# The first two weight items of the feed-forward stage: gate then up, or turn by turn

## The reference

```
x = x + rms_norm(mix, norm_w[1])
h = rms_norm(x, norm_w[2])
ff = (silu(h @ w_gate) * (h @ w_up)) @ w_down      # w_gate, w_up: 1024 x 2816, w_down: 2816 x 1024
x = x + rms_norm(ff, norm_w[3])
```

## Time and profile before

| | |
|---|---|
| median of 3 runs | 2828.58 us (2825.28 to 2828.79) |
| the profiled execution: its time, its span | 2831.39 us, 2829.6 us |
| PE busy | 2705.1 us, 96% of the span |
| DVE, ACT, POOL busy | 1829.3, 1115.9, 1227.8 us |
| granted TensorE clock, mean | 0.973 |

### The profile page before, as it was taken

How to read it: one execution, slowest core, us unless ns; L and a number is a source line. 1 busy time by engine, 2 the same in 40 slices (tenths; PEclk the granted TensorE clock), 3 DMA queues, 4 the chain that set the end, 5 groups by cost and what they waited for, 6 DMA issues and landing times. The chain is left out here.

```text
span 2829.6 us, 36052 instructions
## 1 busy us (share of the span) xinstructions
PE 2705.1 (96%) x12868; PEld 2175.8 (77%) x12868; DVE 1829.3 (65%) x2886; ACT 1115.9 (39%) x2094; POOL 1227.8 (43%) x776
## 2 busy tenths in 40 slices
PE   7999999999799999999989999999997999999997
PEld 5677877778588888888766788777785888888886
DVE  4479865583766566666654798545738656666666
ACT  4336434573523222333333364336744322233323
POOL 1228410340656544565433284103316654466545
PEclk9999999899899999999999999998998999999999
DMA  4103310433111211111330123105231121111113
GB/s 134 45 23 90 112 60 25 141 90 112 38 60 47 73 45 44 46 58 59 128 102 23 31 91 111 60 18 155 90 111 39 53 67 45 44 51 53 59 59 127
DMA packets 186881, 199.30 MB, mean 70 GB/s; under 512 B 19312, under 2 KB 162800, under 8 KB 186496
## 3 DMA queue, kind: packets, MB, share of 16 engines
q1 hardware_dynamic: 180992, 176.63, 20.1%
q10 hardware_dynamic: 5760, 20.97, 1.9%
HBM read 158.78 MB, written 38.80 MB: 70 GB/s over the span
## 5 line engine op out<-in xcount | busy, mean ns | idle before, releaser
L2178 POOL TENSOR_TENSOR ring_lo<-ring_sum,ring_hi 128x512 fp32r<-128x512 f32 x212 | 318.9, 1519 | 500.8 <-ACT ring_hi L2259 500.8
L2395 PE MATMUL ps<-form_hi,ring_hi 128*128 128x512 f32 x1232 | 484.3, 393 | 27.2 <-issue 14.5
L2395 PE MATMUL ps<-form_lo,ring_hi 128*128 128x512 f32 x1232 | 482.5, 392 | 0.0
L2395 PE MATMUL ps<-form_hi,ring_lo 128*128 128x512 f32 x1232 | 482.2, 391 | 0.0
L901 PE MATMUL ps<-act_hi,whi 128*128 128x512 f32 x960 | 395.9, 412 | 9.2 <-ACT smr L441 8.4
L2259 ACT ACTIVATE ring_hi<-ring_sum 128x512 fp32r<-128x512 f32 x212 | 132.7, 633 | 641.1 <-DVE ring_sum L2464 641.1
L901 PE MATMUL ps<-act_lo,whi 128*128 128x512 f32 x960 | 379.2, 395 | 0.0
L901 PE MATMUL ps<-act_hi,wlo 128*128 128x512 f32 x960 | 379.2, 395 | 0.0
L2507 DVE TENSOR_TENSOR yacc<-yacc,ps 128x1024 f32<-128x1024 f32 x176 | 214.8, 1220 | 243.4 <-PE ps L2421 243.4
L1316 DVE TENSOR_SCALAR_CACHE_REDUCE ties<-score,kth 128x384 uint8<-128x384 f32 (+5 forms) x396 | 348.4, 942 | 4.8
L604 POOL TENSOR_TENSOR wlo<-raw,whi 128x1024 fp32r<-128x1024 f32 x56 | 137.1, 2448 | 408.7 <-ACT whi L646 408.7
(11 more groups left out here) (323 smaller groups left out, 4731.3 us busy)
## 6 DMA issues: line engine op xcount, KB each, us to landing
raw<-in_w_in SPq DMA_DIRECT2D x56, 512.0 KB, 3.8
ff_raw<-in_w_gate SPq DMA_DIRECT2D x22, 1024.0 KB, 5.4
ff_raw<-in_w_up SPq DMA_DIRECT2D x22, 1024.0 KB, 5.3
ff_raw<-in_w_down SPq DMA_DIRECT2D x22, 1024.0 KB, 5.1
proj_scratch<-stage ACTq DMA_DIRECT2D x40, 512.0 KB, 2.7
wc<-proj_scratch SPq DMA_DIRECT2D x14, 1280.0 KB, 6.7
xmid_scratch<-xres SPq DMA_DIRECT2D x16, 512.0 KB, 2.6
resid<-xmid_scratch SPq DMA_DIRECT2D x16, 512.0 KB, 6.4
```

The lines of the kernel that those rows point to most:

```text
L2178: pool.tensor_tensor(flat_form(ring_lo[slot]), src, flat_form(ring_hi[slot]).bitcast(F32), ALU.subtract)\
L2395: mm = pe.matmul(ps[:, PRODUCT_BANK[i], :], w[:, k], a[:, k], start=(k == 0 and m == 0), stop=(k == 3 and m == 2))
```

## The change

The first gate item and the first up item become one sequence of fourteen products, `OPENING`, with f as its place: G0, G1, U0, U1, G2, G3, G4, U2, U3, U4, G5, G6, U5, U6 (f = 0 to 13). T7 stands between U0 and U1. The up item has the banks 4 to 7 of PSUM for its products, where the transposes of the tiles are written too (even tiles in 4 and 5, odd ones in 6 and 7): U0 waits for tile 6 to be copied out, U2 for tile 7. Both items take their raw blocks, each from its own buffer. The tables OPENING_SUM, OPENING_DRAIN, OPENING_STEP and OPENING_PIECE give the counts of semaphores for the new order. From H0 on every queue has its old order.

What moves on the other engines:
- DVE sums the weight forms in the order of f, makes `form_lo3` of the earlier tiles itself (POOL did), and drains G1, U1 and G2 between its token forms.
- ACT copies G0 and U0 out before the high parts of the token forms 5 and 6.
- POOL makes fourteen `ring_lo` in the order of f; the zeroing of `yacc` stands after f = 11, and waits for `form_lo6`.
- SP loads the second gate block after twelve `ring_lo`, not seven.

```diff
-            t_lo_p = sig("t_lo_p", 3)
-            t_lo_v = sig("t_lo_v", 7)
+            t_lo_p = sig("t_lo_p", 2)
+            t_lo_v = sig("t_lo_v", 8)
+            TOKENS_READY = {2: 3, 3: 4, 4: 6, 5: 7, 6: 8}
...
+            OPENING = ((0, 0), (0, 1), (1, 0), (1, 1), (0, 2), (0, 3), (0, 4), (1, 2), (1, 3), (1, 4), (0, 5), (0, 6), (1, 5), (1, 6))
+            OPENING_SUM = {(0, 1): 1, (1, 1): 2, (0, 2): 3, (0, 3): 4, (0, 4): 5, (1, 2): 6, (1, 3): 7, (1, 4): 8, (0, 6): 9, (1, 6): 10}
...
+            opening = lambda r: isinstance(r, int) and r < 2
+            summed = lambda r, i: OPENING_SUM[r, i] if opening(r) else 5 * r + SUMMED[i]
+            drained = lambda r, i: OPENING_DRAIN[r, i] if opening(r) else 10 * r + DRAINED[i]
+            step_done = lambda r, n: OPENING_STEP[r][n] if opening(r) else 10 * r + n
+            piece_done = lambda r, n: OPENING_PIECE[r][n] if opening(r) else 10 * r + (1, 7, 8, 10)[n]
+            product_bank = lambda r, i: 4 + PRODUCT_BANK[i] if opening(r) and r == 1 else PRODUCT_BANK[i]
...
+            def first_sum(v, f):
+
+                s, i = OPENING[f]
+                v.wait_ge(*f_in[s](L, 16))
+                if f >= 6:
+                    v.wait_ge(*f_done(L, f - 5))
                 a, b, op = WEIGHT_SUM[i]
-                v.tensor_tensor(flat_form(ring_sum[(i + 5) % 6]), weight_part(ff_raw[0], *a), weight_part(ff_raw[0], *b), op)\
+                v.tensor_tensor(flat_form(ring_sum[(f + 5) % 6]), weight_part(ff_raw[s], *a), weight_part(ff_raw[s], *b), op)\
                  .then_inc(f_sum.sem, 1)
...
                 token_hi(act, 3, LAST)
+                first_form_hi(act, 4)
                 act.wait_ge(*t_sum(L, 5))
                 token_hi(act, 4, LAST)
-                first_form_hi(act, 4)
-                first_form_hi(act, 5)
+                for f in range(5, 8):
+                    first_form_hi(act, f)
+                act.wait_ge(*x_out[0](L, 16 * NT // 2))
+                first_product(act, gate_t, 0, 0)
+                act.wait_ge(*x_out[1](L, 16 * NT // 2))
+                first_product(act, up_t, 2, 1)
+                first_form_hi(act, 8)
                 for i in (5, 6):
                     act.wait_ge(*t_sum(L, i + 1))
                     token_hi(act, i, EVERY)
+                    if i == 5:
+                        first_form_hi(act, 9)
...
-                        for i in range(1, 4):
-                            first_sum(v, i)
+                        first_sum(v, 1)
+                        first_sum(v, 3)
...
                 v.wait_ge(*d_xn(L, NT))
                 first_sum(v, 4)
-                lo(4, EARLIER, 5)
+                lo(3, EARLIER, 4)
                 v.wait_ge(*d_hi(L, NT))
                 token_sum(v, 2, LAST)
                 token_sum(v, 4, LAST)
                 lo(2, LAST, 6)
                 lo(3, LAST, 7)
+                first_sum(v, 5)
+                lo(4, EARLIER, 5)
                 lo(4, LAST, 8)
+                first_sum(v, 6)
+                first_sum(v, 7)
                 token_sum(v, 5, EVERY)
+                drain(v, gate_t, 1, 1, 0)
+                drain(v, up_t, 1, 3, 1)
+                first_sum(v, 8)
                 token_sum(v, 6, EVERY)
+                first_sum(v, 9)
                 lo(5, EVERY, 9)
+                drain(v, gate_t, 2, 4, 0)
                 lo(6, EVERY, 10)
...
+                def loads(k, p):
+                    load_gate(k + 1, 12 if isinstance(k, int) and k == 0 else cycle(k), p)
+                    load_down(k, cycle(k) + 7, 1 - p)
+                    load_up(k + 1, cycle(k) + 14, p)
+
+                for p in range(2):
+                    loads(p, p)
...
-                pool.wait_ge(*t_hi(L, 4))
-                token_lo(pool, 3, EARLIER, t_lo_p)
                 if N < DEPTH:
                     clear_columns(pool)
                 first_form_lo(pool, 4)
                 first_form_lo(pool, 5)
-                form_lo_part(6, 6, 5, (0, 1))
-                pool.wait_ge(*t_lo_v(L, 7))
-                pool.wait_ge(*t_lo_p(L, 3))
-                for t in range(NT):
-                    ins = pool.memset(yacc[t][:, :], 0.0)
-                    if t % 4 == 3:
-                        ins.then_inc(y_add.sem, 1)
-                for j in range(6):
-                    form_lo_part(j, 7 + j, j, (1, 1))
+                for f in range(6, 14):
+                    first_form_lo(pool, f)
+                    if f == 11:
+                        pool.wait_ge(*t_lo_v(L, 8))
+                        for t in range(NT):
+                            ins = pool.memset(yacc[t][:, :], 0.0)
+                            if t % 4 == 3:
+                                ins.then_inc(y_add.sem, 1)
+                hid_lo(0, 0)
+                form_lo_part(0, 14, 1, (0, 2))
+                form_lo_part(1, 15, 2, (0, 2))
+                hid_lo(0, 1)
+                form_lo_part(2, 16, 3, (0, 2))
+                form_lo_part(3, 17, 4, (0, 2))
+                form_lo_part(4, 18, 5, (0, 2))
+                hid_lo(0, 2)
+                form_lo_part(5, 19, 0, (0, 2))
...
                     pe.wait_ge(*f_lo(L, f + 1))
-                    later = not (isinstance(r, int) and r == 0)
+                    later = not opening(r)
+                    last = r - 2 if isinstance(r, int) and r == 2 else r - 1
                     if i == 0 and later:
-                        pe.wait_ge(*m_drain(L, 10 * (r - 1) + DRAINED[4]))
+                        pe.wait_ge(*m_drain(L, drained(last, 4)))
                     if i == 1 and later:
-                        pe.wait_ge(*m_drain(L, 10 * (r - 1) + DRAINED[5]))
...
                 pe.wait_ge(*t_lo_p(L, 2))
                 pe.wait_ge(*d_mix(L, NT - 1))
-                product(0, 0, 5, 0)
-                product(1, 1, 0, 0)
-                turn_normed(pe, NT - 1)
-                pe.wait_ge(*d_mix(L, NT))
-                for i in range(2, 7):
-                    pe.wait_ge(*t_lo_v(L, i + 1))
-                    if i == 3:
-                        pe.wait_ge(*t_lo_p(L, 3))
-                    product(i, i, (i + 5) % 6, 0)
+                for f in range(14):
+                    r, i = OPENING[f]
+                    if f == 2:
+                        pe.wait_ge(*d_hi(L, NT - 1))
+                    if f == 3:
+                        turn_normed(pe, NT - 1)
+                    if f == 4:
+                        pe.wait_ge(*d_mix(L, NT))
+                    if f == 7:
+                        pe.wait_ge(*d_hi(L, NT))
+                    if r == 0 and i >= 2:
+                        pe.wait_ge(*t_lo_v(L, TOKENS_READY[i]))
+                    product(i, f, (f + 5) % 6, r)
...
+                drain(v, gate_t, 3, 5, 0)
+                first_sum(v, 11)
+                drain(v, gate_t, 4, 6, 0)
+                drain(v, up_t, 2, 7, 1)
+                first_sum(v, 13)
+                drain(v, up_t, 3, 8, 1)
+                hid(0, 0)
+                drain(v, up_t, 4, 9, 1)
+                hid(0, 1)
+                form_sum_part(1, 15, 2, (0, 2))
+                drain(v, gate_t, 5, 10, 0)
+                form_sum_part(2, 16, 3, (0, 2))
+                drain(v, gate_t, 6, 11, 0)
+                form_sum_part(3, 17, 4, (0, 2))
+                drain(v, up_t, 5, 12, 1)
+                form_sum_part(4, 18, 5, (0, 2))
+                hid(0, 2)
+                drain(v, up_t, 6, 13, 1)
+                hid(0, 3)
                 for p in range(2):
                     turn_of(p, 0, p)
```

More of the change, by code:

```diff
@@ L1494, in turn_bank @@
                 return ps[:, 4 + 2 * (t % 2):6 + 2 * (t % 2), :].rearrange("p a b -> p (a b)")
+            e_par = sig("e_par", 16)
+            m_first = sig("m_first", 2 * FB)
+            m_drain = sig("m_drain", 10 * 2 * FB)
+            silu = sig("silu", 4 * FB)
+            hidden = sig("hidden", 4 * FB)
+            h_hi = sig("h_hi", 4 * FB)
+            h_lo = sig("h_lo", 4 * FB)
+            y_ps = sig("y_ps", NT * FB)
+            e_stat = sig("e_stat", 3 * NT)
+            e_yn = sig("e_yn", NT)
@@ new lines, in layer @@
+            e_in = [sig(f"e_in{s}", 16 * NT // 2) for s in range(2)]
+            e_end = sig("e_end", 2)
+            last_bank = lambda t: ps[:, 0:2, :].rearrange("p a b -> p (a b)") if t % 2 == 0 else turn_bank(1)
+            STAT_X, STAT_Y = 64, 76
+            N = L + 1
+            cycle = lambda k: 7 + 18 * k
+            up_item = lambda k: 2 * k + 1
+            gate_item = lambda k: 2 * k + 2
+            up_place = lambda i, p: (1, 3 * i + 1) if p == 0 else (0, 3 * i + 3)
+            gate_place = lambda i, p: (0, 3 * i + 2) if p == 0 else (1, 3 * i + 3)
@@ new lines, in drain, with add, copy @@
+            def drain(v, t, i, f, r):
+                src = ps[:, product_bank(r, i), :]
+                def add(quarter, op, after):
+                    q = quarter_of(t, *quarter)
+                    if after:
```

(39 more changed lines are left out.)

236 lines of the change are left out of this document (92 added, 144 removed).

## The result

| | before | after |
|---|---|---|
| median of 5 runs each, same chip | 2828.58 us | 2811.12 us (2810.47 to 2814.2) |
| ratio, with its 95% interval | | 0.9942 (0.9922 to 0.9961) |
| profiled execution: time, span | 2831.39, 2829.6 us | 2814.2, 2812.4 us |
| PE, DVE, ACT, POOL busy | 2705.1, 1829.3, 1115.9, 1227.8 us | 2694.6, 1822.2, 1115.7, 1231.5 us |

The account below looks back on a forecast made before the run. PE, busy 96%, was the bound, with only idle and low-clock time to win. H0 moving from 790.1 to 783.0 gives 7.1 us a layer, 14.2 in all: 2817.2 profiled, 2814.4 us median; 8-in-10 range 2805 to 2823.

Parts of the forecast that it names:

- 1: At tile 6 DVE keeps two of three sums: statistics 2.2 us earlier (724.8), T7 at 735.7, one 0.8 us POOL wait.
- 2: U0 fills PE before T7, 731.5 to 734.2; T7 waits 1.5 us, not 5.49, and runs at full clock.
- 3: `form_lo3` on DVE adds 1.67 us but stops holding DVE's sum (3.91 us); G2 starts at 743.5, before 746.41.
- 4: From 735.6 DVE is the bound: 25.7 us of work, 3.7 meeting POOL, 0.4 for ACT; G6's sum ends at 765.4.
- Rivals A: DVE hardly meets POOL and PE runs U5 at 2.4 GHz: gain 12.2 us a layer, 2804 us; chance 0.12.
- B: All eight meetings of DVE with POOL cost 1.25 us each: gain -0.4 us a layer, 2829 us; chance 0.06.
- 5: On POOL, f = 11 and then 7.2 us of zeroing (to 774.6) hold back U5's form, f = 12, until 776.1.
- 6: On PE, G4 waits 1.9 us and U5 5.7; 1.4 us added for low clock; H0 at 783.0.
- 7: Taken as free: second gate block landing at 773.6, ACT, PSUM banks, and POOL before `down` (0 to 2.1 us).
- Rival C: POOL's 17 subtractions before `down` take 1.74 us each: 2.1 us late, gain 5.0 a layer, 2818.6 us; counted within range.
- Rival D: PE, fed one product at a time from G2 on, stays at 1.2 GHz: slower, 2838.6 us; chance 0.05.
- Rival E: In the new order the up products need something not ready: gain 0, within 0.2%; chance 0.04.

Follow-up runs that it names:

- x8: The changed kernel once more, unchanged; median 2811.33 us, ratio 0.9951.
- x4: The kernel before with only G3's weight sum, with its high and low part, moved behind the last tile's norm; median 2829.17 us, ratio 1.0004.
- x6: The changed kernel with T7 put ahead of U0 on PE, not after it; median 2813.64 us, ratio 0.9947.
- x5: The changed kernel with `form_lo3` of the earlier tiles made by POOL again, not DVE; median 2815.2 us, ratio 0.9962.
- x1: The changed kernel without the zeroing of `yacc`, the first `down` product being copied instead of added; median 2796.47 us, ratio 0.9901.
- x9: The changed kernel without the zeroing, plus 15 unread matmuls in PE's wait ahead of G2; median 2798.93 us, ratio 0.9896.
- x7: The kernel before once more, unchanged; median 2831.07 us.
- x10: The changed kernel without the zeroing of `yacc`, run once more; median 2793.36 us, ratio 0.9893.
- x3: The changed kernel with 20 unread matmuls between G6 and U5, inside PE's wait; median 2808.87 us, ratio 0.9944.

## Why the prediction was right

The forecast was 2814.4 us, the median is 2811.12 (x8: 2811.33). The mechanism is the one it named, and the yardstick H0 starts at 783.68 - 0.69 = 782.99 us, where it said 783.0. Step by step:

1. The last tile's statistics start at 725.44 - 0.69 = 724.75 (724.8 said), T7 at 735.52 (735.7). The one meeting with POOL that the step allowed 0.8 us for is there: `form_sum2` takes 2.63 us (a form of that size takes 1.75), 0.9 us more. x4 shows that this step moves T7. Made alone it moves neither G2 nor U0; its 1.5 us of stretch are U0's clock.
2. T7 waits 1.07 us (1 to 2) and runs at full clock. True, but x6 shows that it is no term of the gain: its place decides nothing.
3. G2 at 743.26 (743.5). x5: without this step the stretch is 2.6 to 2.8 us longer, so it is the largest single part that I could take out.
4. DVE's queue from 736.07 to the end of G6's sum, 765.40, lasts 29.3 us; 29.8 were said (25.7 of work, 3.7 of meetings, 0.4 of ACT). Rivals A (no meetings) and B (all eight in full) put that at 26.1 and 36.1 us, so both are out. The sum of the meetings was right, not their picture: DVE lost three of them, about 1.1 us each (the rows of 742.60, 744.28 and 756.23), and in most of the others POOL waited (3.44 us for its 128x512 at 761.32, against 1.26 at 774.56).
5. The zeroing ends at 774.6 - 0.7 = 773.9 (774.6), f = 12 at 775.1 (776.1), held by POOL alone as said. x1 shows the cause. The 1.8 us that zeroing would take if it held DVE did not come: it took 7.22 us, and DVE's `up_t` product with both inputs in SBUF took 0.68 us beside it (769.12).
6. Two errors of about one us cancel, which is luck. U5 starts 1.0 us earlier than said, and the slow steps behind its wait cost 783.68 - 775.88 - 2 x 2.73 = 2.3 us, where 1.4 had been taken from a shorter wait (3.42 us). The term that failed is that 1.4: the wait was known to be longer, and the row was not scaled. By the same reckoning the row itself is 1.6 us, not 1.4: H0 of before, 84 matmuls behind U0's first, starts at 790.3, not the 790.1 of the forecast, so the measured gain to H0 is 7.3 us a layer, 7.1 said. G4's wait of 1.9 us is missing too: G2 ran cold and used it up; G3 started 0.9 us later than said, where the step allowed 0.6 at most. x9 brings G4's wait back, 2.03 us, when PE is warm.
7. The second gate block held DVE for 1.61 us and PE for none: PE has no wait between 783 and 830 us. The first matmul of `down` starts at 802.7 - 0.7 = 802.0 (802.1).

Rival C needed POOL to be late for `down`; it wasn't. Rival D needed the clock to stay down: it was 1.00 from 750 to 770 us. Rival E falls with T7's and G2's starts.

The median fell by 17.5 us, the stretch by 14.7 where the scans agree (14.2 forecast). The rest, 2.8 us, is within the interval of the ratio, and I put it down to the scan stages, whose code is unchanged and which take from 98 to 105 us a layer from one execution to the next.

**What stays open** is why they do. It isn't the order of the opening: x4 and x7 differ in it only by one sum and have first scans of 98.4 and 105.0 us, ahead of that sum; x1 and x10 are the same kernel, with 105.0 and 98.4. It is not separated either what U0 and U1 ahead of G2 give and what U2 to U4 ahead of G5 give.

## What to carry to other kernels

When two independent streams each wait for their own forming, let them take turns, but look at what each queue is made to do between the last item that is early and the first that is late: here a 7.2 us zeroing, harmless by busy time, took back 3.0 of 10.3 and 3.6 of 11.0 us a layer until the first addition became a copy. Where the queue that forms the operands was the bound, a full clock or an earlier start on PE was worth nothing (x9, x6); a fill of PE's idle time paid only where PE itself was what was late next (x3 yes, x9 no). Where a price is read off a wait, scale it to the wait that will be there.
